# Maxima over partitions by ones-products ahead of the MLP loop of a GLA and Fourier layer, and a later clear of the MLP sums

## The reference

```python
h = _rmsnorm(x, g_pre_mix) * (1 + sc_m) + sh_m          # shift, scale, gate from silu(c) @ w_ada
z = h @ w_in                                            # q | k | v | g | low rank fwd | bwd | u
o_f, s_f = _gla_chunked(q, k, v, la_f, s0_fwd)          # gated linear attention, both directions
o = _rmsnorm(o_f + flip(o_b), g_head) * jax.nn.silu(g)
y = jnp.concatenate([o, _fourier_mix(u)], axis=-1) @ w_out
x = x + gt_m * _rmsnorm(y, g_post_mix)
h = _rmsnorm(x, g_pre_mlp) * (1 + sc_f) + sh_f
f = jnp.square(jax.nn.relu(h @ w_fc1)) @ w_fc2
x = x + gt_f * _rmsnorm(f, g_post_mlp)
```

## Time and profile before

| | |
|---|---|
| three runs | 1483.51, 1487.07 and 1493.52 us, median 1487.07 |
| profiled execution | span 1476.2 us from the first to the last instruction (its own time is not given beside it) |
| PE / DVE / ACT / POOL busy | 1252.9 / 747.0 / 425.2 / 256.6 us |
| mean granted clock of TensorE | 0.928 of full speed |
| DMA | 97.24 MB, mean 66 GB/s |

### The profile page before, as it was taken

The page is one execution under the profiler, slowest core; times in us unless marked ns, Lnnn a source line. Parts: engine busy times, 40 slices in busy tenths (PEclk is TensorE's granted clock), DMA queues, the critical chain, the costliest instruction groups (busy, mean ns, idle before and its releaser), DMA issues.

```text
span 1476.2 us, 18755 instructions
## 1 busy us (share of the span) xinstructions
PE 1252.9 (85%) x7319; PEld 736.4 (50%) x7319; DVE 747.0 (51%) x1093; ACT 425.2 (29%) x736; POOL 256.6 (17%) x416
## 2 busy tenths in 40 slices
PE   3449999999862338976879999999999999999995
PEld 2225568886651314433445454454554545546442
DVE  3364583892652434755545444444545354454537
ACT  4354352322111215643333032130311312213103
POOL 1111120430212111112211111202112111121104
PEclk9779999999785768988989999999999999999998
DMA  9822011434300220000011110101011010111003
GB/s 294 266 92 63 29 58 37 147 112 147 118 29 0 105 109 29 1 14 16 29 57 34 54 57 30 58 30 57 32 55 58 29 57 29 58 39 48 29 0 128
DMA packets 70751, 97.24 MB, mean 66 GB/s; under 512 B 3077, under 2 KB 53386, under 8 KB 70666
## 3 DMA queue, kind: packets, MB, share of 16 engines
q1 hardware_dynamic: 70666, 96.04, 19.9%
HBM read 86.33 MB, written 9.70 MB: 65 GB/s over the span
## 4 chain that ended last, share of the span: by engine, by line
PE 47%; issue 2%; DVE 1%; POOL 1%; ACT 1%; POOLq 0%; ACTq 0%; DVEq 0%
PE bank L1202 47%; ACT bank L866 1%; POOL region L833 1%; DVE region L2055 0%; POOL small L757 0%; DVE region L2026 0%; POOL small L677 0%; DVE region L1953 0%; DVE ghb L1953 0%; ACT whi L554 0%; DVE region L2057 0%; DVE region L1942 0%; POOL small L755 0%; ACT region L1115 0%; ACT region L1120 0%
## 5 line engine op out<-in xcount | busy, mean ns | idle before, releaser
L1202 PE MATMUL bank<-region,whi 128*128 128x384 f16 (+1 forms) x1872 | 460.4, 328 | 47.8 <-issue 31.9
L1202 PE MATMUL bank<-whi,region 128*128 128x512 f16 (+1 forms) x1872 | 487.9, 348 | 8.9 <-DVE region L1909 8.9
L1202 PE MATMUL bank<-wlo,region 128*128 128x512 f16 (+1 forms) x936 | 325.3, 348 | 0.0
L1202 PE MATMUL bank<-region,wlo 128*128 128x384 f16 (+1 forms) x936 | 307.2, 328 | 0.0
L1202 PEld LDWEIGHTS bank<-region,whi 128*128 128x128 f16 (+1 forms) x1872 | 183.3, 98 | 174.5 <-issue 37.8
L1202 PEld LDWEIGHTS bank<-whi,region 128*128 128x128 f16 x1872 | 184.2, 98 | 170.5 <-DVE region L1909 9.8
L1202 PE MATMUL bank<-region 128*128 128x512 f16 (+8 forms) x802 | 176.0, 386 | 64.0 <-DVE region L1858 34.3
L2026 DVE SCALAR_TENSOR_TENSOR region<-bank,small,region 128x512 f32<-128x512 f32 x144 | 106.7, 749 | 180.5 <-PE bank L1202 180.1
L554 ACT ACTIVATE whi<-stage,small 128x2048 f16<-128x2048 f32 (+1 forms) x42 | 82.3, 1960 | 338.3 <-PE bank L1202 291.1
L1202 PEld LDWEIGHTS bank<-region 128*128 128x128 f16 (+4 forms) x802 | 112.7, 171 | 119.5 <-issue 48.2
L702 POOL PARTITION_ALL_REDUCE small<-small x45 | 76.3, 1695 | 407.1 <-DVE small L537 335.1
(11 more groups left out here) (152 smaller groups left out, 900.7 us busy)
## 6 DMA issues: line engine op xcount, KB each, us to landing
stage<-in_w_fc SPq DMA_DIRECT2D x32, 1024.0 KB, 5.2
stage<-in_w_ada SPq DMA_DIRECT2D x16, 1024.0 KB, 5.3
region<-in_w_ada SPq DMA_DIRECT2D x8, 1024.0 KB, 12.0
stage<-in_w_in SPq DMA_DIRECT2D x8, 1024.0 KB, 5.4
x_with_position<-region SPq DMA_DIRECT2D x9, 512.0 KB, 4.9
region<-x_with_position SPq DMA_DIRECT2D x9, 512.0 KB, 9.1
out_dram<-region SPq DMA_DIRECT2D x9, 512.0 KB, 2.6
region<-in_x_sample SPq DMA_DIRECT2D x8, 512.0 KB, 10.6
```

Of the source, the lines that this page charges most:

```text
L1202: return nc.tensor.matmul(out, lhsT, rhs, start=start, stop=stop, skip_group_check=True)
```

## The change

For the stages ahead of the MLP loop the maximum over partitions is no longer taken by POOL. PE multiplies the 128 one-column maxima by a matrix of ones into bank 7, so that every partition holds the sum of the 128 maxima, an upper bound in place of the maximum, and DVE divides it, forms the factor and takes a reciprocal. In three places, the bound of h for the MLP and the first two W1 chunks, PE first turns the column into a row, DVE takes the true maximum of the row, and a product with a row of ones spreads it. The list `peaks` numbers these 22 sums and row turns in PE's order, and a new pair of semaphores hands bank 7 back and forth. POOL keeps its reduces for the other 30 MLP chunks. The throwaway squares go to SBUF buffers that nobody reads at that time; one of the four diagonal buffers moves. POOL's scale of the first chunk of the second MLP group goes ahead of the clear of `acc`.

```diff
+    peaks = [("w", 0), ("h", 0)] + [("w", i) for i in range(1, len(zin))]
+    peaks += [("w", w0), ("w", w0 + 1), ("row", "h", 1), ("h", 1), ("y", 1), ("w", w0 + 2), ("y", 0), ("w", w0 + 3)]
+    peaks += [("row", "w", F), ("w", F), ("row", "w", F + 1), ("w", F + 1)]
...
-        junk = banks[7]
+        peak_sum, peak_row = banks[7][:, 0:1], banks[7][0:1, 0:P]
...
-        diag = tb2 + [gex[:].rearrange("p b n -> p (b n)"), R34[:, 8704:9216]]
+        diag = tb2 + [R34[:, 4096:4608], R34[:, 8704:9216]]
...
             for j in range(NT):
                 x_rstd(j)
-            chunk_scale(0, False)
             A.take(pool, ada1[6])
             nc.gpsimd.memset(wa2, 0.0).then_inc(s_wa2, 1)
-            h_scale(0)
-            for i in range(1, len(zin)):
-                chunk_scale(i)
...
-                if s == 6:
-                    y_scale(1)
-                if s == 8:
-                    chunk_scale(len(zin) + 2, False)
-                if s == 4:
-                    h_scale(1)
-                    chunk_scale(len(zin), False)
-                    chunk_scale(len(zin) + 1, False)
...
-            y_scale(0)
-            for c in range(3):
-                chunk_factor(len(zin) + c)
-            chunk_scale(len(zin) + 3, False)
-            chunk_factor(len(zin) + 3, s_cof)
...
+            ff_up_scale(1, 0)
             A.take(pool, ("wo", 3, NT - 1))
             A.take(pool, A0 + 5)
             nc.gpsimd.memset(acc, 0.0).then_inc(s_accz, 1)
-            ff_up_scale(1, 0)
...
-                    nc.scalar.activation(junk[:, 0:width], src[:, width * h:width * h + width], ACT.Square,
+                    nc.scalar.activation(unread[:, 0:width], src[:, width * h:width * h + width], ACT.Square,
...
+            def sum_peaks(key):
+                n = peak_no[key]
+                kind, i = key[-2:]
+                if kind == "w":
+                    pe.wait_ge(s_wmax, i + 1)
+                    cols_ = [wmax[:, i % 8:i % 8 + 1]]
...
+                if key[0] == "row":
+                    ins = mm(peak_row, cols_[0], ident, True, True)
+                elif ("row",) + key in peak_no:
+                    ins = mm(peak_sum, ones[0:1, :], top_peak[0:1, :], True, True)
+                else:
+                    for m, col in enumerate(cols_):
+                        ins = mm(peak_sum, ones, col, m == 0, m == len(cols_) - 1)
+                ins.then_inc(s_pk, 1)
...
+                    if i == LR and n == 1:
+                        sum_peaks(("w", 1))
+                    if n == (2 if i == LR else 3):
+                        sum_peaks(("w", i + 2))
...
+                if s in (4, 5, 7):
+                    sum_peaks({4: ("w", w0), 5: ("row", "h", 1), 7: ("w", w0 + 2)}[s])
                 outputs(s, j)
+                if s in (4, 5, 6):
+                    sum_peaks({4: ("w", w0 + 1), 5: ("h", 1), 6: ("y", 1)}[s])
...
+            def peak_inverse(key, out, factor=1.0):
+                n = peak_no[key]
+                dve.wait_ge(s_pk, n + 1)
+                V.tensor_scalar(out, peak_sum, factor / TOP, TINY, ALU.mult, ALU.max).then_inc(s_pkr, 1)
+                dve.wait_ge(s_pkr, n + 1)
...
+            def chunk_scale(i, factor=True):
+                c = slice(i % 8, i % 8 + 1)
+                peak_inverse(("w", i), winv[:, c])
+                if factor:
+                    chunk_factor(i)
+                V.reciprocal(wscl[:, c], winv[:, c]).then_inc(s_wscl, 1)
...
                 if r == 1:
                     chunk_max(dve, 1)
+                if r == 3:
+                    chunk_scale(1)
...
             for i in range(G_A):
                 chunk_max(dve, i + 2)
                 chunk_low(dve, i + 1)
...
+                chunk_scale(i + 2)
...
+                if s == 4:
+                    chunk_scale(w0, False)
+                if s == 5:
+                    peak_top(("h", 1))
+                if s == 7:
+                    chunk_scale(w0 + 2, False)
                 gate_o(s, j)
...
             chunk_low(dve, w0 + 2)
+            chunk_scale(w0 + 3, False)
+            chunk_factor(w0 + 3, s_cof)
             for q in range(4):
                 diagonals(q)
             chunk_low(dve, w0 + 3)
...
+                if j in (5, 6):
+                    peak_top(("w", F + j - 5))
                 if j + 2 < NT:
                     low_y(j + 2)
...
                 if j < NT:
                     put_odd(3, j)
+                if j in (5, 6):
+                    chunk_scale(F + j - 5, False)
```

111 lines of the change are left out of this document (72 added, 39 removed).

## The result

The changed kernel took 1362.82 us (median of four runs, 1361.6 to 1363.83), the kernel before 1485.29 (four runs beside it, 1482.99 to 1493.52): a ratio of 0.9183 with a 95% interval of 0.9152 to 0.9213, faster by 122 us. Forecast were 1374 us, 1346 to 1406.

The account below looks back on a forecast made before the run. The prediction took PE's idle time, behind POOL's reduces, to bound the kernel. Terms -17 - 63 - 23 - 11.3 + 1 = -113 on the span of 1476.2, plus 10.9 around it, gave 1374 us, range 1346 to 1406.

Parts of the forecast that it names:

- What bounds the kernel: Whole kernel: gains come from PE's idle time, at most 223 us, caused by POOL's reduces; MLP loop unchanged.
- The price of the replacement: Each replaced reduce: product, hand-over and two DVE steps take 1.0 us (0.5 to 2.3) against some 15 before.
- Term 1: The start: gains scaled 20 us earlier, some given back; -17 us, between -20 and -12.
- Term 2: Attention to W_out: gates no longer wait behind POOL's reduces; -63 us (-50 and -13), between -87 and -45.
- Term 3: W_out to the MLP: two long PE waits and half clock go, 3 us given back; -23, between -26 and -14.
- Term 4: Second MLP group's first chunk: its reduce goes ahead of POOL's clear of the sums; -11.3 us, between -13 and -4.
- Squares: Throwaway squares ahead of the loop, into SBUF: 13 ns more each for some 90; +1 us, between 0 and +3.
- Half of it comes back: Rival: PE and DVE wait for each other, 2.4 us lost at each of 22 products; 1427 us, chance 0.10.
- The full price, slower than before: Rival: PE held at each of 22 products, 5.8 us a product; slower by over 1%, chance 0.02.
- no change: Rival: the new path costs as much as the old, 14 us like the reduce; 1487 us, chance 0.02.
- More than the sum: Rival: all five waits of attention to W_out go, other terms reach their ends; -146, 1341 us, chance 0.07.

Follow-up runs that it names:

- experiment 7: Changed kernel with each product that sums or turns the maxima issued four times instead of once; 1379.2 us.
- the second profile: The changed kernel profiled and timed once more, unchanged, on another chip; 1360.8 us.
- experiment 2: Changed kernel with the maxima of the first two W1 chunks formed by all-reduces on POOL again; 1378.2 us.
- experiment 5: Kernel before with one edit, the all-reduce for up(1,0) put ahead of the clear of the sums; 1473.7 us, ratio 0.992.
- experiment 1: Changed kernel with the all-reduce for up(1,0) put back behind the clear of the sums; 1370.4 us.
- experiment 8: Kernel before with one edit, the unread squares written to SBUF instead of a PSUM bank; 1486.6 us, ratio 1.0013.
- experiment 10: Changed kernel with two all-reduces of an unread column added on POOL in every round of the MLP loop; 1366.1 us.
- experiment 11: Changed kernel with DVE's scale of the gains held until POOL has done two added all-reduces of an unread column; 1366.8 us.
- experiment 3: Changed kernel with the maxima of the nine W_in chunks and the first norm's gains formed on POOL again; 1391.4 us.

## Why the prediction was right, step by step

**What bounds the kernel** held: the time came out of PE's idle stretches, POOL's reduces were their cause, and the loop behind them kept its length (739.8 to 740.5 us from up(0,1) in every changed kernel without the clear first).

**The price of the replacement**, 1.0 us for a round trip, was 1.1 at the start. The product was put at 0.26 us, and experiment 7 gives 0.29 where nothing hides it and 0.07 where waits do.

**Term 1**, -17: measured -19.4 in the stage table. The gains came 20.8 us earlier against the last part (forecast 20), and 1.4 were given back (forecast 3); DVE's wait for the low-rank tile was 1.75 us, expected 1. The gains came at 67.36 and not "near 60 us", by the late start alone. Undone, the start was worth 28.5, of which 8.3 lie in W_in in the profiled execution, mostly as drops of the clock. These did not come in the profile of before, and the term could not hold them.

**Term 2**, -63: -49.5 and -15.0, so -64.5; undone 63.4. The last gate was put near 457 and came at 458.89. The steps were forecast at 13.6, 11, 11, 11 and 5 and came at 13.6, 11.6, 9.6, 12.2 and 5.2. "No wait over 5 us between the first and the last gate" failed: the sum for chunk w0+2 cost 6.62, which is the price of the maximum "for which PE now waits in its order", put at a part of 1.6. In the second profile the five steps took 54.6 us, not 52.2, so single steps are known to some 2 us. The -4.5 ahead of it was not forecast; experiment 2 shows the longer form of this stretch in a kernel with the new code, so it was not the change.

**Term 3**, -23: -20.1, and 16.7 undone. Too large by 3 to 6 us: the 3 us given back were 6, of which 2.5 are PE's wait for the maximum of the first W1 chunk, 1.5 the half clock in the 3 us behind it (545.31 to 548.31), and 1.2 the longer waits of the turns (3.3 in all against the 2.1 that the two short ones of before took). That leaves 1.0 for the products and all else.

**Term 4**, -11.3: 11.2 in experiment 5 and in the stage of experiment 1. The table's -14.0 holds 2.9 us of two waits of PE put to "issue" in the loop of before (1.54 and 1.36), which the changed kernel had for 0.2. Experiments 5 and 8, the other two with the kernel before's loop, have them too (2.2 and 2.7 us), and no changed kernel does; what they are was not settled.

**Squares**, +1: nothing measurable, though a square takes 28 ns more and not 13.

**The step that failed** is the last: "the median of the three runs, 1487.07, lies 10.9 above, and I take that as what lies around the span". In every run with both numbers the time is 1.7 to 2.2 us above the span (1363.83 and 1362.0; for before 1480.74 and 1478.9). The profiled execution of before thus took about 1478 us: it was a quick one, with an early start and no drop of the clock in W_in. So 1476.2 - 113 + 1.8 = 1365 would have been the sum for an equally lucky execution, and the profile after was less lucky by 8.3 us at its start.

That the forecast missed by only 11 us has luck in it. The last step was 9 us too high. The terms were 9 us too small: without its first row the stage table gives -122.5 where -113 was forecast (4.5 of it in the first gates, 2.7 in the loop's last row, 2.4 in term 1). Both put the forecast too high, and the late start of the profile after, 8.3, which no term held, took one of them back. The mechanism does not rest on this luck, since each part was undone by itself. A slip of the range: its shallow end adds up to 1415, not 1414.

**Rivals.** Half of it comes back: the waits for a maximum or for the read of a sum are some 15 us in 22 sums, 0.7 each and not 2.4. Of the 22 only three waits are of 2 us and more (6.6, 3.2 and 2.5). The full price, slower than before, and no change are out with it. More than the sum is out too, though not by much: of the 122 us some 9 were forecast by no term.

## What to carry to other kernels

A cross-partition reduce that is off the busy engine can still set the pace by what stands behind it in its queue. Price it by the idle time around its row, not by the row, and ask for each use what waits for the next instruction on that engine. When such a step goes to engines that run in order, place it where its input is long done: five sums placed earlier than that cost some 4 us here. And before a sum is set against a profile, look at whether the profiled execution is a typical one: here its span lay 9 us further below the median of the runs than the fixed 1.8 us, more than any of the four terms was off.

## What the runs showed of the hardware that was not expected

A reduce over partitions on POOL is recorded with 0.35 to 0.4 us in most places ahead of the loop, and with 2.4 us in 27 of the 30 of the changed kernel's loop, all of which stood waiting for DVE's maximum. The 5.7 us ahead come once for a run of reduces, and the idle time behind comes at the next arithmetic, not at a clear (experiments 10 and 11). Over all runs it is 6.7 to 8.4 us behind most of the short ones and 8.7 to 10.0 behind nearly all of the long ones (in the earlier trace rows one stood alone, with 6.17 and 7.65). So the kernel before could have put its reduces side by side; that was not tried.

PE's granted clock fell to its lower level in W_in while PE's record shows it busy all the time, and each of these drops began in or right behind twelve fp32 products on 32 partitions; half of the runs of such products passed without one (experiment 3 and the profiles named there). What decides between the two was not settled.
